# Memory's projections laid behind other products, the last down products by token groups, and a gate product in the LRU's last step

## The reference

```python
h = rmsnorm(x, W['norm_mix'])
u = h @ W['w_in']                        # all branches' inputs and the gates' logits
y_lru, ... = rg_lru_branch(...);   b_lru = y_lru @ W['w_lru_out']
...                                      # GLA branch -> b_gla, SSD branch -> b_ssd
gates = sigmoid(gate_logits)             # three gates of width 1024
x = x + (gates[0] * b_lru + gates[1] * b_gla + gates[2] * b_ssd) @ W['w_mix_out']
mn = rmsnorm(mem, W['norm_mem'])         # 256 memory tokens
k, v = mn @ W['w_xk'], mn @ W['w_xv']    # outputs too; samples use caches instead
x = x + cross_attention(rmsnorm(x, W['norm_xattn']), k, v, W['w_xq'], W['w_xo'])
h = rmsnorm(x, W['norm_ffn'])
x = x + (silu(h @ W['w_ffn_gate']) * (h @ W['w_ffn_up'])) @ W['w_ffn_down']
y = rmsnorm(x, norm_final)
```

## Time and profile before

| | us |
|---|---|
| median of 3 runs (3059.91 to 3061.11) | 3060.51 |
| the profiled execution | 3061.23 |
| its span, first to last instruction | 3059.5 |
| TensorE busy | 2922.0 (96%) |
| VectorE busy | 1239.4 (41%) |
| ScalarE busy | 695.1 (23%) |
| GpSimd busy | 847.4 (28%) |
| mean granted TensorE clock | 0.98 |

### The profile page before, as it was taken

The page is one execution under the profiler, slowest core; times in us unless marked ns, Lnnn a source line. Parts: engine busy times, 40 slices in busy tenths (PEclk is TensorE's granted clock), DMA queues, the critical chain, the costliest instruction groups (busy, mean ns, idle before and its releaser), DMA issues.

```text
span 3059.5 us, 41382 instructions
## 1 busy us (share of the span) xinstructions
PE 2922.0 (96%) x17754; PEld 2743.3 (90%) x17754; DVE 1239.4 (41%) x1884; ACT 695.1 (23%) x1243; POOL 847.4 (28%) x501
## 2 busy tenths in 40 slices
PE   7999999999999999989988998898999999999997
PEld 6998999797988899977758998887999999999997
DVE  5886102324232247428843302234153333333335
ACT  3554001223121112215522113024020000000003
POOL 3232232112212133233412333301233232332320
PEclk9999999999999999999989999999999999999998
DMA  3111222212121433232233333142111111111111
GB/s 111 42 35 38 71 64 62 67 37 70 40 68 55 160 123 85 62 90 80 79 93 133 114 90 99 58 155 92 42 41 43 43 48 42 49 42 49 42 45 70
DMA packets 300247, 216.36 MB, mean 71 GB/s; under 512 B 30747, under 2 KB 279644, under 8 KB 300066
## 3 DMA queue, kind: packets, MB, share of 16 engines
q1 hardware_dynamic: 225602, 132.21, 15.4%
q10 hardware_dynamic: 74464, 81.50, 8.1%
HBM read 172.96 MB, written 40.73 MB: 70 GB/s over the span
## 4 chain that ended last, share of the span: by engine, by line
PE 88%; DVE 6%; ACT 3%; DMA 1%; issue 1%; POOL 1%; SPq 0%; ACTq 0%; DVEq 0%; POOLq 0%
PE PS L734 53%; PE PS L1394 8%; PE PS L750 6%; PE PS L790 3%; DVE WK L2203 3%; PE PS L774 2%; PE PS L798 2%; PE PS L1191 1%; PE PS L1097 1%; PE PS L1073 1%; PE PS L813 1%; PE PS L1253 1%; PE PS L1277 1%; PE PM L941 1%; PE PS L957 1%
## 5 line engine op out<-in xcount | busy, mean ns | idle before, releaser
L734 PE MATMUL PS<-Hh,Wh 128*128 128x384 f32 (+1 forms) x2928 | 963.9, 329 | 8.3 <-ACT WK L1431 6.8
L734 PE MATMUL PS<-Hh,Wl 128*128 128x384 f32 (+1 forms) x2928 | 959.0, 328 | 0.0
L734 PE MATMUL PS<-Hl,Wh 128*128 128x384 f32 (+1 forms) x2928 | 958.7, 327 | 0.0
L674 POOL CAST Wh<-Wr 128x1024 fp32r<-128x1024 f32 x205 | 241.8, 1180 | 1945.3 <-DMA Wr<-in_w_in 817.9
L734 PEld LDWEIGHTS PS<-Hh,Wh 128*128 128x128 f32 x2928 | 553.4, 189 | 10.4 <-issue 9.3
L734 PEld LDWEIGHTS PS<-Hl,Wh 128*128 128x128 f32 x2928 | 553.2, 189 | 0.6
L734 PEld LDWEIGHTS PS<-Hh,Wl 128*128 128x128 f32 x2928 | 553.0, 189 | 0.0
L676 POOL TENSOR_TENSOR Wl<-Wr,Wh 128x1024 fp32r<-128x1024 f32 x213 | 535.3, 2514 | 53.8 <-ACT Wh L2013 37.3
L2203 DVE SCALAR_TENSOR_TENSOR WK<-WK,PS 128x384 f32<-128x384 f32 x186 | 98.4, 532 | 614.7 <-PE PS L734 433.1
L2825 DVE TENSOR_TENSOR X<-X,PS 128x384 f32<-128x384 f32 (+1 forms) x288 | 147.5, 529 | 157.8 <-PE PS L1394 80.9
L734 PE MATMUL PS<-Yh,Wh 128*128 128x384 f32 (+1 forms) x576 | 189.1, 328 | 4.8 <-DVE Yl L2500 4.8
(11 more groups left out here) (418 smaller groups left out, 4125.4 us busy)
## 6 DMA issues: line engine op xcount, KB each, us to landing
Wr<-in_w_in SPq DMA_DIRECT2D x82, 512.0 KB, 3.9
Wr<-in_w_ffn_gate SPq DMA_DIRECT2D x22, 512.0 KB, 3.8
Wr<-in_w_ffn_up SPq DMA_DIRECT2D x22, 512.0 KB, 3.8
Wr<-in_w_ffn_down SPq DMA_DIRECT2D x22, 512.0 KB, 3.7
merged<-WK ACTq DMA_DIRECT2D x16, 544.0 KB, 4.0
WK<-gates ACTq DMA_DIRECT2D x16, 544.0 KB, 4.9
WK<-merged ACTq DMA_DIRECT2D x16, 544.0 KB, 6.0
Wr<-in_w_lru_out SPq DMA_DIRECT2D x8, 512.0 KB, 4.4
```

The costliest lines, as they stand in the source:

```text
L674: pool.tensor_copy(Wh[:, n % SLOTS], Wr[:, n % SLOTS]).then_inc(w_hi, 1)
L734: mm = pe.matmul(bank(f"{name}:{g}")[:, 0:n], L[:, w % SLOTS, k, :], R[:, k, t0:t0 + n], start=(k == 0 and i == 0), stop=(last and k == DT ...
```

## The change

- **Gate product.** `og0_0` moves from the head of `out_jobs(0)` into the LRU's step 7, ahead of `lr7` and `li7`, where the other steps have `lx`. ScalarE makes its tanh there, behind the square of the gate branch and ahead of `lr7`'s; the buffers of the gates swap parity.
- **Memory's norm.** `memory_root` in step 0 of `out_jobs(2)`, `scale_memory` ahead of VectorE's step 0, the turning behind `ob2_0`, the weighing in step 0. The parts `MAh`, `MAl` are made in step 1, in the place of tiles 6 and 7 of `Hh` and `Hl`. After `ob2_7` they are copied to `MNh`, `MNl`, and only then are tiles 6 and 7 of the sum's parts made.
- **Memory's products.** The sixteen stand one behind each of `ob2_2` to `ob2_6`, `mx0` to `mx7`, `xq1` to `xq3`. `kt0` and `kt1` are turned behind `mx1` and `mx3`, `vt0` behind `mx7`, `vt1` behind `xq4`. GpSimd makes both parts of V's weights too. The sums of squares of x go into `PM`, between steps of xq0 and xq1 by tile, as the feed-forward has it; roots and reciprocals follow there. Buffers move accordingly (`XT`, `KM`, `KT_m`, `VF`, `PrT`, `SQ`).
- **The end.** `fd10` runs group by group: eight tiles of group 0, of group 1, of group 2. A token tile is turned as soon as its tokens are done: in groups 1 and 2 one behind t = 2, 4 and 6, the last three at the end. Their banks are fixed in pairs (`OWN_BANK`). ScalarE squares each turned tile with a sum per row and takes the root, VectorE takes the reciprocal and scales and weighs in one pass for each half, SyncE stores. The final gain is loaded as rows by ScalarE's queue before the feed-forward, and is no longer among the vectors at the start (`NPACK` 17 for 18).

```diff
+MEM_JOBS = [(kind, t) for kind in ("mk", "mv") for t in range(DT)]
+MEM_BEHIND = [f"ob2_{t}" for t in range(2, DT - 1)] + [f"mx{t}" for t in range(DT)] + [f"xq{t}" for t in range(1, 4)]
+MEM_JOB = dict(zip(MEM_BEHIND, MEM_JOBS))
...
+LAST = {(g, 2 + 2 * i): 3 * (g - 1) + i for g in (1, 2) for i in range(3)}
+OWN_BANK |= {f"yt{_c}:{_a}": 2 * (_c % 3) + _a for _c in range(TT + 1) for _a in range(2)}
...
+        else:
+            use([("in", C_GATE)], "og0_0")
...
+        def turned(c):
+            b = JOB[f"yt{c}:0"][0]
+            return PS[0:P if c < TT else TS, b:b + 2, :]
...
-                sp.dma_start(wk(0)[R_NFIN:R_NFIN + 1, 0:D], I["norm_final"].unsqueeze(0)).then_inc(packs, 16)
...
+            for c in range(TT + 1):
+                y = O["y_prompt"][0, c * P:(c + 1) * P] if c < TT else O["y_sample"].rearrange("b l f -> (b l) f")
+                read(sp, f"yt{c}:0")
+                read(sp, f"yt{c}:1")
+                sp.dma_start(y, Out(c)).then_inc(S("out"), 16)
...
-                    if WLIST[n][0] != "xv":
-                        pool.tensor_copy(Wh[:, n % SLOTS], Wr[:, n % SLOTS]).then_inc(w_hi, 1)
+                    pool.tensor_copy(Wh[:, n % SLOTS], Wr[:, n % SLOTS]).then_inc(w_hi, 1)
...
+            def project_memory(behind, Rh, Rl):
+
+                if behind not in MEM_JOB:
+                    return
+                kind, t = MEM_JOB[behind]
+                name, w = f"{kind}{t}:0", FIRST_W["x" + kind[1], t * P]
+                pe.wait_ge(w_split, w + 1)
+                pe.wait_ge(S("mem_hi"), 2 if Rh is MAh else 3)
+                pe.wait_ge(S("mem_lo"), 2 if Rh is MAh else 3)
...
-                    if b == 2 and t == 3:
-                        turn_memory(0)
-                        turn_memory(1)
+                    if b == 2:
+                        if t == 0:
+                            turn_memory(0)
+                            turn_memory(1)
+                        project_memory(f"ob2_{t}", MAh, MAl)
...
+            project_by_tile(("xq0", "xq1"), FIRST_W["xq", 0], ("nrm_lo", 0),
+                            {3: lambda: sum_norm(0, (0, 1)), 5: lambda: sum_norm(0, (2,))})
+            for t in range(1, DT):
+                if t > 1:
+                    project(f"xq{t}", FIRST_W["xq", t * P], Hh, Hl)
+                project_memory(f"xq{t}", MNh, MNl)
                 if t == 4:
...
+                    turn_kv("vt1", VF, f"mv{DT - 1}")
...
+            for g in range(len(GROUPS)):
+                for t in range(DT):
+                    down(FC - 1, t, g)
+                    if (g, t) in LAST:
+                        turn_result(LAST[g, t])
+            for c in range(GROUPS[-1][0] // P, TT + 1):
+                turn_result(c)
...
+                        if b == 2:
+                            if t == 0:
+                                memory_root()
+                            if t == 1:
+                                mem_hi()
+                            if f"ob2_{t - 1}" in MEM_JOB:
+                                copy_product(f"ob2_{t - 1}")
...
+                ready(act, f"ob2_{DT - 1}:2")
+                act.wait_ge(S("mem_lo"), 2)
+                act.activation(MNh[:], MAh[:], ACT.Copy).then_inc(S("mem_hi"), 1)
+                act.wait_ge(S("mem_hi"), 3)
+                hi_sum(DT - 2)
                 hi_sum(DT - 1)
...
+                else:
+                    all_groups("og0_0", wk(1), ACT.Tanh, scale=0.5)
...
+                if t == DT - 1:
+                    hi_scaled(0, R_NX)
+                    copy_turned_kv("vt0", MV[:, :, 0:512])
+                copy_product(f"mx{t}")
...
+                link(act.activation(wk(4 + c % 2)[0:n, 0:D].rearrange("p (a f) -> p a f", a=2), turned(c), ACT.Square,
+                                    accum_out=st))
+                act.activation(st, st, ACT.Sqrt, bias=EPSC[0:n], scale=1.0 / D).then_inc(S("nrm_std"), 1)
...
+                if b == 2:
+                    scale_memory()
                 for t in range(DT):
...
+            dve.tensor_copy(MNl[:], MAl[:]).then_inc(S("mem_lo"), 1)
...
+            def scale_result(c):
+                n = P if c < TT else TS
+                dve.wait_ge(S("nrm_std"), 6 + c + 1)
+                st = ST[0:n, c:c + 1]
+                link(dve.reciprocal(st, st))
+                for a in range(2):
+                    name = f"yt{c}:{a}"
+                    freed(stt(Out(c)[:, 512 * a:512 * a + 512], bank(name)[0:n], st, GAIN_OUT[0:n, 512 * a:512 * a + 512],
+                              MUL, MUL), name)
...
+                    if late is not None and (g, t - 1) in LAST:
+                        scale_result(late)
+                        late = None
```

More of the change, by code:

```diff
@@ L131, in out_jobs @@
         for t in range(DT):
-            if b == 0:
+            if b == 0 and t:
                 use([("in", C_GATE + b * D + t * P)], f"og{b}_{t}")
             use([(name, t * P)], f"ob{b}_{t}")
-            if b == 2 and t == 3:
-                banks("mt0", 2)
-                banks("mt1", 2)
+            if b == 2:
+                if t == 0:
+                    banks("mt0", 2)
+                    banks("mt1", 2)
+                memory(f"ob2_{t}")
     use([("in", C_LX)], "lx0")
@@ L203, in plan @@
         use([("mix", t * P)], f"mx{t}")
[L204 to L213, removed]
+        if t == DT - 1:
             banks("vt0", 2)
-    banks("vt1", 2)
+        memory(f"mx{t}")
+        if t in (1, 3):
+            banks(f"kt{t // 2}", 2)
     for t in range(DT):
         use([("xq", t * P)], f"xq{t}")
+        memory(f"xq{t}")
+        if t == 4:
+            banks("vt1", 2)
     banks("xs0", 2)
@@ L1175, in _ @@
             out_jobs(2, "ssd_out")
[L1176 to L1193, removed]
             def turn_kv(name, src, last):
@@ L1397, in _, with down @@
-            pe.wait_ge(S("nrm_sum"), NSUM * 3)
-            for c in range(TT + 1):
-                n = P if c < TT else TS
-                mm = pe.matmul(PM[0:n, 0, c:c + 1], SQ[:, c * P:c * P + n], ones[:, 0:1], start=True, stop=True)
-            mm.then_inc(S("nrm_mm"), 1)
-            for c in range(TT + 1):
+            def down(e, t, g):
+                name = f"fd{e}_{t}"
+                w = FIRST_W["fd", (e, t // 4)]
+                t0, n = GROUPS[g]
+                pe.wait_ge(w_split, w + 1)
+                free_bank(pe, f"{name}:{g}")
+                for k in range(2):
+                    for i, (L, R) in enumerate(((Wh, Fh), (Wh, Fl), (Wl, Fh))):
+                        lhsT = L[:, w % SLOTS].rearrange("p (k a) m -> p k (a m)", k=2)[:, k, t % 4 * P:(t % 4 + 1) * P]
+                        mm = pe.matmul(bank(f"{name}:{g}")[:, 0:n], lhsT, R[:, e % 2, k, t0:t0 + n],
+                                       start=(k == 0 and i == 0), stop=(k == 1 and i == 2))
+                done(mm, f"{name}:{g}")
@@ L2041, in _ @@
+            roots(0)
+            for t in range(1, 4):
+                copy_product(f"xq{t}")
             copy_turned_kv("vt1", MV[:, :, 512:D])
-            for m in range(2):
-                read(act, f"vt0:{m}")
-                read(act, f"vt1:{m}")
+            for i in range(4):
+                read(act, f"vt{i // 2}:{i % 2}")
             store(O["p_mem_v"][0, 0].rearrange("(m p) h d -> p m (h d)", p=P), MV)
-            n_kv[0] = n_stores[0]
+            act.wait_ge(S("mem_in"), 32)
```

327 lines of the change are left out of this document (150 added, 177 removed).

## The result

| | before | after |
|---|---|---|
| median, us (range) | 3060.65 (3059.91 to 3061.11) | 3040.85 (3038.77 to 3045.94) |
| the profiled execution | 3061.23 | 3039.03 |
| its span | 3059.5 | 3037.3 |

The account below looks back on a forecast made before the run. TensorE, busy 2922.0 of 3059.5 us, was taken as the bound, so only its gaps and the slow clock after them could be won. Terms −0.3 − 4.3 + 7.7 − 14.3 − 6.5 = −17.7 from 3061.2 gave 3043.5 us, range 3033 to 3054.

Parts of the forecast that it names:

- Part 2: Gate product og0_0 in the LRU's last step: ob0_0 effectively starts earlier despite a 3.5 us wait, −4.3 us.
- Part 1: Start: one row less on SyncE's queue ahead of the vectors TensorE waits for, −0.3 us.
- Part 3: Memory's norm at the head of ob2: TensorE waits 4.9 us for scaled rows and loses clock, +7.7 us.
- Part 4: Memory's products among ob2, mx and xq: same product cost, fewer gaps, waits before xq0 and xq2, −14.3 us.
- Part 5: The end, fd10 by token groups with tiles turned between jobs: −6.5 us, bounds −9 and 0.
- about 23 us: Sign at the end: the span ends this long behind the last fd10 matmul of group 1.
- The forecast's own case: Whole kernel: the summed terms hold, giving 3038 to 3050 us; chance 0.55.
- (b): Shorter waits before ob0_0, xq0 and xq2 and at the end, clock not lowered: 3034.7 us; chance 0.15.
- (a): Gaps come back: waits before xq0 and xq2 near doubled, or ob0_0's gain nil: 3053.5 us; chance 0.20.
- (c): Slower token-tile chain at the end, 7.5 us per extra us; table loads each time give 3067; chance 0.06.
- (d): Memory's products hide nothing, each waiting for its own weight tile: about 3061 us; chance 0.04.
- a wait of over 8 us before mt: Sign of being wrong, at memory's transposes behind ob2_0, where a wait of about 5 us was expected.

Follow-up runs that it names:

- e1: The changed kernel once more, with no edit: 3048.51 us, ratio 0.9940 to the kernel before.
- e2: Changed kernel with each og0 gate product one product further ahead, og0_1 standing before ob0_0: 3035.94 us, ratio 0.9905 to the kernel before.
- e3: Changed kernel with memory's rows scaled in step 1 and turned behind ob2_1 instead of ob2_0: 3036.85 us, ratio 0.9906 to the kernel before.
- e4: Changed kernel with memory's last three V products behind xq2, xq3 and xq3 instead of xq1, xq2 and xq3: 3044.67 us, ratio 0.9926.
- e7: Changed kernel with og0_0 put back at the head of out_jobs(0), its tanh with it: 3046.49 us, ratio 0.9947 to the kernel before.
- e6: Changed kernel with each turned tile at the end squared twice on ScalarE: 3054.86 us, ratio 0.9977 to the kernel before.
- e8: Changed kernel with the edits of e2, e3, e4 and e5 together: 3025.5 us, ratio 0.9877 to the kernel before.
- e5: Changed kernel with the end's banks given out in ring order and turns behind t = 1, 3 and 5: 3042.42 us, ratio 0.9932.

## Why the prediction was right, and where its terms were not

The mechanisms all came: the wait on y's low half, the wait on memory's scaled rows, none on memory's weights, one before xq0 and one before xq2, waits on VectorE in the last group, one function table for square and root. The sum was −17.7, the profiles differ by 22.2 and the medians by 19.8. That the number is so near is partly luck: Part 2 gained 2.1 us less than forecast, Parts 3, 4 and 5 came out 1.2, 2.2 and 3.9 us better, and the stretches that nobody touched, +4.3 and −3.2, happened to cancel in this profile.

- **Part 1** (−0.3) can't be told: the stretch up to the small products of step 6 is −0.7 to +1.1 in nine profiles of the same code.
- **Part 2** (−4.3, measured −2.2 in after, −2.7 in the mean). The sizes were off in two steps. From the end of lr7's tanh to the end of y's low half I took 17.5 us over from before; it is 18.4 (271.84 to 290.20). And I priced a gap of 3 to 4 us at 1.7 of clock: ob0_0 took 14.87 for 11.86, 3.0 lost. In e1, with the same wait, it lost 1.7. So the price of such a gap is a spread, not one number.
- **Part 3** (+7.7, measured +6.5, mean of seven +8.2). The root was expected 3.0 after ob2_0's end, and came so (1653.17). VectorE's scalings were expected at 1.5 us: 1.42. The wait was 4.7 for 4.9, and the clock took 1.8 (the turns, 3.55 for 1.75) where I had 2.8. This held since the split came later than the scaling, and the next section shows what happens when it doesn't.
- **Part 4** (−14.3, measured −16.5, mean −16.7). The waits were 3.9 and 4.0 for 4.8 and 3.8; the first is smaller because GpSimd's high and low part took 3.5 us and not 4.8. From mx7's end to xq7's end it is 122.6 for 123.7. The other 1.1 is the price of memory's products: 2.88 us each in ob2, where I had 3.07 from a row in which the product stood between other work. No slot was late, and the order between ob2_7 and mx0 cost nothing, as counted.
- **Part 5** (−6.5, measured −8.8 to −10.4). The failed step is when a bank comes free. I let the waiting job stand until both of VectorE's passes are through; its bank is the first of the pair and is given back after the first, 0.7 us sooner. From the start of the turn to the next job it is 3.5 us (3014.97 to 3018.51) for 4.4, so the last group waits 4.2 us in all, for 7.1 expected. And I added 1.5 for a lower clock, where after had none. The 24 jobs and nine turns took 32.6 for 31.7, and behind TensorE's last turn (it ends at 3029.45) it is 7.8 us for 8.4. The "about 23 us" between group 1's last matmul and the end doesn't follow from the prediction's own terms, which give 28.9 (from fd10's start at 3004.5, 16 jobs and three turns end at 3024.0, and the span at 3052.9); it is 25.1.
- **The stretches that aren't touched** (0, measured +4.3 and −3.2 in after). They had no term and are the largest error of any single line. Two pieces of the GLA branch's stage in before and then in after, with the same operations (busy time by stretch):

```profile
523.67:609.75 86.08, 82.83 (x526) 66.33 (x525) 24.75 (x62) 15.49 (x43) 16.40 (x10) 0.99 0.24 70
878.90:1015.99 137.09, 129.75 (x809) 114.09 (x808) 44.82 (x91) 34.03 (x66) 26.33 (x16) 0.99 0.19 56
```

```profile
520.79:608.50 87.71, 84.53 (x527) 67.13 (x525) 24.75 (x62) 15.48 (x43) 16.93 (x10) 0.97 0.24 69
877.70:1017.53 139.83, 132.50 (x807) 116.86 (x808) 44.83 (x91) 34.02 (x66) 25.85 (x16) 0.96 0.18 54
```

VectorE's and ScalarE's busy time is the same to 0.01 us, TensorE's waits in them are the same to 0.1 us, and TensorE is busy 1.7 and 2.8 us longer at a mean clock of 0.97 and 0.96 for 0.99. So nothing of the change shows in these two pieces; only the clock falls low for longer. Between xq7 and fd10 it is the other way round: idle times of 19.6 and 19.5 us, and the clock low for 13.7 us in before and for 3.4 in after.

**The rule on transposes.** In the last group of after the clock was 1.00 among turns and waits. The Trainium skill has it that transposes don't count as TensorE's busy time as matmuls do and don't bring the full clock (TensorE: Matmul & The Clock Gate, "PE-mode transpose"). The prediction worked out from it a group at the low level and 3 us more; the traces of after, e2 and e3 disagree. In e1, e4 and e7 the last turn and the last job of the group did run slow, for 1.3 to 1.6 us more from fd10 to the end. The mean of the six is 0.7 us, where I had put 1.5.

**The rivals.** The forecast's own case, 3038 to 3050, came. (b), shorter waits, is what the end did and the wait before xq0. (a) was half right for ob0_0. (c) had its price about right: I worked out 7.5 us, without the clock, for each us on the chain of a token tile, and e6 measured 8 to 9.4 with it (6.8 in waits and behind the last matmul). Its condition was absent. The ground given against it was a little off: at the start of before the first square and the first root do load a table each (at 3.3 and 6.8 us), and only the later ones there do not. At the end of after the table is loaded once, for the first tile's root (ScalarE):

```profile
3006.25 1.28 ACT L2217 ACT_TABLE_LOAD   x1
3007.55 0.29 ACT L2217 ACTIVATE ST<-ST,EPSC 128x1 f32<-128x1 f32 x1
```

(d) did not come: no memory product waited.

## What to carry to other kernels

A wait is best removed by putting work that is needed anyway in front of it, and the wait that a move creates behind itself is worth as much thought as the one it takes away: shifting two steps by one more product each gave back nearly all that the new waits cost (e2, e3). Price a gap of some 4 us of TensorE as the gap and a spread of 1.6 to 3 us behind it (ob0_0 and xq2 in the eight kernels with such a wait). Judge a small change by its own stretch between two points of the order, since stretches that it doesn't touch moved by up to 9 us from one profile to another.

## What the runs showed of the hardware

**The same code, nearly the same waits, another clock.** From ob0_0's end to ob2's start all these kernels do the same (e2 and e8 with each og0 one product ahead). The time at the low level between 300 and 1640, worked out from the traces, beside the length of this stretch less that of before:

| | before | e7 | e8 | e3 | e2 | e5 | e1 | after | e6 | e4 |
|---|---|---|---|---|---|---|---|---|---|---|
| us at the low level | 64.9 | 64.9 | 64.9 | 64.9 | 68.3 | 68.3 | 71.7 | 75.1 | 75.1 | 78.5 |
| stretch, us more | 0 | −0.3 | −0.1 | 0.2 | 1.4 | 0.8 | 2.8 | 4.3 | 4.4 | 7.0 |

Where the low time grows by 7 to 14 us, each us of it costs 0.4 to 0.5 us, and the amount differs between runs by 13.6 us. TensorE's idle time in the stretch is 52.4 to 53.9 us in the ten profiles, so waits explain at most 1.5 of the 7 us, and 0.7 of e4's. No edit explains the rest. What decides it stays open; I didn't try to steer it.

**Two operations on one port.** Memory's two scalings are the same instruction everywhere, and took 1.42, 2.19 and 4.09 us in after, e1 and e5. VectorE and GpSimd in order of time, in these three:

```profile
1653.41 1.42 DVE L2243 TENSOR_SCALAR WK<-WK,ST 128x1024 f32<-128x1024 f32 x2
1654.18 1.54 POOL L710 CAST Wh<-Wr 128x1024 fp32r<-128x1024 f32 x1 [8.04 <-DMA Wr<-in_w_xk]
```

```profile
1651.62 2.19 DVE L2243 TENSOR_SCALAR WK<-WK,ST 128x1024 f32<-128x1024 f32 x2
1652.06 1.21 POOL L710 CAST Wh<-Wr 128x1024 fp32r<-128x1024 f32 x1 [7.72 <-DMA Wr<-in_w_xk]
```

```profile
1651.03 1.04 POOL L720 CAST Wh<-Wr 128x1024 fp32r<-128x1024 f32 x1 [7.85 <-DMA Wr<-in_w_xk]
1652.15 2.67 POOL L722 TENSOR_TENSOR Wl<-Wr,Wh 128x1024 fp32r<-128x1024 f32 x1
...
1651.28 4.09 DVE L2253 TENSOR_SCALAR WK<-WK,ST 128x1024 f32<-128x1024 f32 x2
```

Where GpSimd's cast starts 0.8 us later than the scalings, they take 1.42; where it starts 0.25 us earlier, 2.7 more, and the wait at the head of ob2 is 8.3 us for 4.7 (0.9 of it because the data landed later). The trace has the two scalings apart: each takes 0.75 us by itself. In e1 the second ends at 1653.82, 0.55 us after the cast's end; in e5 it ends at 1655.37, 0.55 us after the subtraction's. So it stood until GpSimd's instruction was through. This is what the Trainium skill says of the shared pair (SBUF — State Buffer, "shared port pair": the loser blocks for the whole instruction). By it the prediction put a split that starts first at 2.6 us more and Part 3 at +10.3; the scalings agree (2.7 more), while the +10.0 of e5 is partly luck, since the data came 0.9 us later and the clock took 1.7 us where the prediction had 2.8. A few tenths in when the two start decide: of the seven kernels with this order one had 1.42 (the cast 0.77 us behind), one 4.09 (0.25 us ahead), and five 2.19 to 2.28 (0.40 to 0.69 us behind). The prediction named a wait of over 8 us before mt as a sign of being wrong; it didn't come in after, but it came in e5.
